# A two-block fp32 transformer kernel: ffn output halves, index order, 128-row queries, out product by token, and fp32r maxima

## The reference

```
ffn:   h = (silu(n @ w_gate) * (n @ w_up)) @ w_down        # hidden width 2816
       x = x + 0.5 * rms_norm(h, g)
mlstm: dmat[t, s] = b[t] - b[s] + i[s], -inf for s > t     # chunks of 128 tokens, 8 heads
       m[t] = max(b[t] + m_prev, max_s dmat[t, s]); p = (q k^T) * exp(dmat - m)
mix2:  p = rms_norm(x) @ w_in, split into conv (cb, cc, cx, cgate), q, k, v, agate,
           iq, ik, iw, pool (pu, pgate) and three gates of width 1024 (mgate)
       q, k = rope(rms_norm per head); iq, ik = rope
       score[t, s] = sum_h relu(iq_h[t] . ik[s] / 8) * iw[t, h] / sqrt(8), -inf for s > t
       keep the 64 largest scores of each token; softmax(q k^T / 8) over the kept keys, 8 heads of 64
       merged = sum_b sigmoid(mgate_b) * (y_b @ w_out_b); x = x + merged @ w_o
```

## Time and profile before

| | |
|---|---|
| median of 3 runs (range) | 1643.65 us (1642.29 to 1644.79) |
| the profiled execution: time, span | 1644.14 us, 1642.4 us |
| TensorE / VectorE / ScalarE / GpSimd busy | 97% / 59% / 49% / 3% of the span |
| DMA | 279.23 MB, mean 170 GB/s |
| chain that ended last, by engine | PE 76%, DVE 14%, ACT 5%, issue 2% |

### The profile page before, as it was taken

How to read it: one execution, slowest core, us unless ns; L and a number is a source line. 1 busy time by engine, 2 the same in 40 slices (tenths; PEclk the granted TensorE clock), 3 DMA queues, 4 the chain that set the end, 5 groups by cost and what they waited for, 6 DMA issues and landing times.

```text
span 1642.4 us, 19449 instructions
## 1 busy us (share of the span) xinstructions
PE 1595.2 (97%) x7539; PEld 1305.7 (80%) x7539; DVE 976.2 (59%) x1229; ACT 811.2 (49%) x1018; POOL 54.5 (3%) x97
## 2 busy tenths in 40 slices
PE   7999999899999999999999999999999999999999
PEld 6888778778887788878887888787788878778887
DVE  4555567665555645466666544567945556794564
ACT  5444465363444544456755443554355436436452
POOL 2000010000000000000000000100000000100000
PEclk9999999999999999999999999999999999999999
DMA  9644753255447463554355545563523545443443
GB/s 296 215 155 160 250 193 103 66 203 172 160 148 262 167 203 112 201 190 168 140 167 174 185 153 179 184 224 135 180 87 144 208 165 205 154 154 103 154 155 127
DMA packets 189093, 279.23 MB, mean 170 GB/s; under 512 B 8509, under 2 KB 102885, under 8 KB 189024
## 3 DMA queue, kind: packets, MB, share of 16 engines
q1 hardware_dynamic: 186752, 271.27, 47.6%
q0 software_dynamic: 2128, 6.97, 1.6%
q10 hardware_dynamic: 144, 0.03, 0.0%
HBM read 277.20 MB, written 1.06 MB: 169 GB/s over the span
## 4 chain that ended last, share of the span: by engine, by line
PE 76%; DVE 14%; ACT 5%; issue 2%; DMA 1%; POOL 1%; POOLq 0%; SPq 0%; ACTq 0%; DVEq 0%
PE ACC L770 20%; PE ACC L772 20%; PE ACC L771 20%; DVE WL L1953 5%; ACT WH L1352 2%; PE TB L801 2%; PE ZB L946 2%; PE ACC L1075 2%; PE ACC L1077 1%; PE ACC L1076 1%; ACT XH L1383 1%; PE ACC L978 1%; PE ACC L980 1%; PE ACC L979 1%; DVE IS L2467 1%
## 5 line engine op out<-in xcount | busy, mean ns | idle before, releaser
L1953 DVE TENSOR_TENSOR WL<-RAW,WH 128x2048 fp32r<-128x2048 f32 (+2 forms) x258 | 512.2, 2028 | 263.8 <-ACT WH L1352 263.8
L770 PE MATMUL ACC<-WL,XH 128*128 128x512 f32 (+2 forms) x1312 | 516.9, 394 | 20.0 <-issue 6.5
L772 PE MATMUL ACC<-WH,XL 128*128 128x512 f32 (+2 forms) x1312 | 507.1, 387 | 0.0
L771 PE MATMUL ACC<-WH,XH 128*128 128x512 f32 (+2 forms) x1312 | 506.7, 386 | 0.0
L1352 ACT ACTIVATE WH<-RAW 128x2048 fp32r<-128x2048 f32 (+2 forms) x258 | 425.7, 1701 | 154.8 <-PE ACC L772 100.4
L770 PEld LDWEIGHTS ACC<-WL,XH 128*128 128x128 f32 x1312 | 247.5, 189 | 79.5 <-issue 19.8
L772 PEld LDWEIGHTS ACC<-WH,XL 128*128 128x128 f32 x1312 | 247.3, 189 | 50.7
L771 PEld LDWEIGHTS ACC<-WH,XH 128*128 128x128 f32 x1312 | 247.8, 189 | 46.1
L770 PE MATMUL ACC<-WL,HH 128*128 128x512 f32 x352 | 138.3, 393 | 0.9 <-DVE WL L1953 0.4
L772 PE MATMUL ACC<-WH,HL 128*128 128x512 f32 x352 | 137.1, 389 | 0.0
L771 PE MATMUL ACC<-WH,HH 128*128 128x512 f32 x352 | 137.0, 389 | 0.0
(11 more groups left out here) (311 smaller groups left out, 1810.9 us busy)
## 6 DMA issues: line engine op xcount, KB each, us to landing
RAW<-w_in_in SPq DMA_DIRECT2D x66, 1024.0 KB, 6.7
RAW<-ffn_w_gate_in SPq DMA_DIRECT2D x43, 1024.0 KB, 5.2
RAW<-ffn_w_up_in SPq DMA_DIRECT2D x43, 1024.0 KB, 7.4
RAW<-ffn_w_down_in SPq DMA_DIRECT2D x32, 512.0 KB, 4.5
RAW<-ffn_w_down_in SPq DMA_DIRECT2D x16, 1024.0 KB, 6.2
RAW<-mlstm_w_in_in SPq DMA_DIRECT2D x16, 1024.0 KB, 6.9
RAW<-ffn_w_down_in SPq DMA_DIRECT2D x16, 768.0 KB, 6.1
RAW<-attn_w_in_in SPq DMA_DIRECT2D x12, 1024.0 KB, 7.0
```

What stands on the lines that cost most here:

```text
L770: nc.tensor.matmul(bank, lh, wl[:, i, :], start=first and i == 0, stop=False)
L771: nc.tensor.matmul(bank, lh, wh[:, i, :], start=False, stop=False)
L772: mm = nc.tensor.matmul(bank, ll, wh[:, i, :], start=False, stop=last and i == k - 1)
L1953: nc.vector.tensor_tensor(WL[:, slot, lo:hi], RAW[:, slot, lo:hi], WH[:, slot, lo:hi].bitcast(F32), ALU.subtract).then_inc(lo_ready, 1)
```

## The change

- ffn: `scaled` of the first output half (both tiles), and its squares, now stand before the split of chunk 6 (`postnorm_front`).
- `next_x` stands at `k - 3` of the last product instead of `k - 1` (ffn) and `k - 2` (attention, mLSTM); tile 1's transposes at `k - 3` instead of `k - 2`.
- index: the head sums of q (`norms`) and the tasks index 0 and 1 come before q's rotation. `select(1)` is cut into two tasks of four rounds, at slots 16 and 18.
- mix2 queries go to QZ2, one head per 128 rows with the other head's 64 rows zero (zeroed by GpSimd once), by four half-height evacuations instead of two; QT2 shrinks to KT2. The mask is added by VectorE into UL2, from which maxima and exponent read; PE waits for the maxima, no longer for the exponent, before the next scores.
- mix2 out product: token tile 0 of both halves is finished first, with `next_x` in two parts within tile 1; splits and adds follow in `out_tail`.
- mLSTM: MU is split into MUH and MUL on ScalarE and VectorE; identity and `after` are copied to fp32r (IDR, AFR); three fp32r matmuls take the place of two fp32 ones.

The diff without context, indentation reduced:

```diff
@@ -212,15 +212,18 @@
-QT2 = sb("QT2", [P, 3, 4, SEQ], offset=o)
-o += 3 * 4 * SEQ * 4
+KT2 = sb("KT2", [P, 2, 4, SEQ], offset=o)
+o += 2 * 4 * SEQ * 4
+UL2 = sb("UL2", [P, 2, 3 * P], offset=o)
+o += 2 * 3 * P * 4
+QZ2 = sb("QZ2", [P, HEADS, SEQ], offset=sbuf_at["G"])
-MK = sb("MK", [P, 3 * P], F32R, offset=o)
+MK = sb("MK", [P, 3 * P], offset=o)
...
@@ -434,15 +443,15 @@
-task(8, ("rotate", "q"))
+task(8, ("norms", "q"), ("index", 0), ("index", 1), ("rotate", "q"))
-task(12, ("rotate", "k"))
+task(12, ("norms", "k"), ("rotate", "k"))
-for h in range(HEADS):
+for h in range(2, HEADS):
-task(18, "conv_in")
+task(18, "conv_in", ("select", 2))
@@ -599,8 +608,7 @@
-by_half = stages[stage - 1][0] == "mix2"
-return 4 * (stage - 1) + (2 * half + tok if by_half else 2 * tok + half) + 1
+return 4 * (stage - 1) + 2 * tok + half + 1
@@ -752,7 +760,7 @@
-if fresh is not None and tok == 0 and i == k - 2:
+if fresh is not None and tok == 0 and i == k - 3:
@@ -763,7 +771,7 @@
-if tail and tok == NTOK - 1 and i == k - 1:
+if tail and tok == NTOK - 1 and i == k - 3:
@@ -777,9 +785,9 @@
-def of_x(tok, t):
-    for half in range(2):
+def of_x(tok, t, halves=range(2)):
+    for half in halves:
@@ -825,19 +833,12 @@
-def out_product(second_half=None, tok_major=False):
-    if second_half is None:
-        for half in range(2):
-            product(XH, XL, at.chunk, at.chunk % 2, at.block, at.block % 2, 0, KD, COLS, True, True,
-                    tail=next_x if half else None)
-            at.chunk += 1
-            at.block += 1
-        return
+def out_product(second_half):
-    def quarter(part, half, tok, x_at):
+    def quarter(part, half, tok, x_at=None):
@@ -848,31 +849,27 @@
+    t = slice(tok * P, (tok + 1) * P)
-        t = slice(tok * P, (tok + 1) * P)
-        if half and tok and k == x_at:
-            next_x()
+        if x_at and k in x_at and at.stage < len(stages):
+            of_x(0, at.group, (x_at[k],))
-    elif tok and half == 0 and tok_major:
+    elif tok and half == 0:
-        quarter(0, half, tok, None)
+        quarter(0, half, tok)
-if tok_major:
-    for tok in range(NTOK):
-        for half in range(2):
-            quarter(1, half, tok, KD - 2)
-else:
-    for half in range(2):
-        for tok in range(NTOK):
-            quarter(1, half, tok, KD - 1)
+quarter(1, 0, 0)
+quarter(1, 1, 0)
+quarter(1, 0, 1, {KD - 4: 0, KD - 1: 1})
+quarter(1, 1, 1)
@@ -940,12 +937,10 @@
-def head_scores(q, k, z, add=None):
+def head_scores(q, k, z):
-        mm = nc.tensor.matmul(z[:, lo:hi], q[:, queries], k[:, 0:hi - lo], start=True, stop=add is None)
-        if add:
-            mm = nc.tensor.matmul(z[:, lo:hi], add[0], add[1][:, lo:hi], start=False, stop=True)
+        mm = nc.tensor.matmul(z[:, lo:hi], q[:, queries], k[:, 0:hi - lo], start=True, stop=True)
@@ -997,7 +992,7 @@
-if half and tok and k == KD - 2:
+if half and tok and k == KD - 3:
...
@@ -1156,7 +1151,7 @@
-pe.wait_ge(gates_dve, 5)
+pe.wait_ge(largest_lo, 1)
@@ -1168,9 +1163,11 @@
-nc.tensor.matmul(m, ident[:, h:h + 1].broadcast_to([P, P]), MU[:, :], start=True, stop=False)
-nc.tensor.matmul(m.rearrange("p (c t) -> p c t", c=2), ident,
-                 after.unsqueeze(1).broadcast_to([P, 2, P]), start=False, stop=True).then_inc(z_ready, 1)
+of_head = IDR[:, h:h + 1].broadcast_to([P, P])
+nc.tensor.matmul(m, of_head, MUL[:, :], start=True, stop=False)
+nc.tensor.matmul(m, of_head, MUH[:, :], start=False, stop=False)
+nc.tensor.matmul(m.rearrange("p (c t) -> p c t", c=2), IDR[:, :],
+                 AFR[:, :].unsqueeze(1).broadcast_to([P, 2, P]), start=False, stop=True).then_inc(z_ready, 1)
@@ -1234,7 +1231,7 @@
-head_scores(QT2[halves(h), 2, h // 2, :], IKT[halves(h), :], (ZB, OB)[h % 2][:, 0:3 * P]).then_inc(index_z_ready, 1)
+head_scores(KT2[halves(h), 1, h // 2, :], IKT[halves(h), :], (ZB, OB)[h % 2][:, 0:3 * P]).then_inc(index_z_ready, 1)
@@ -1242,11 +1239,10 @@
-    pe.wait_ge(mask_ready, layer + 1)
+    pe.wait_ge(query_rows_zeroed, 2)
-    pe.wait_ge(w_ready, u0 + s)
-head_scores(QT2[halves(s), 0, s // 2, :], QT2[halves(s), 1, s // 2, :], ZB[:, 0:3 * P],
-            (IDR[:, :], MK)).then_inc(z_ready, 1)
+    pe.wait_ge(logits_ready, u0 + s)
+head_scores(QZ2[:, s, :], KT2[:, 0, s // 2, :], ZB[:, 0:3 * P]).then_inc(z_ready, 1)
...
@@ -1419,17 +1415,14 @@
-def postnorm(chunks_per_half):
-    for half in range(2):
-        b = at.block - 2 + half
-        c = at.chunk - 1 - (1 - half) * chunks_per_half
-        for tok in range(NTOK):
-            if half and tok:
-                next_x()
-            block_ready(tok, c, b)
-            square(ACC[:, pair(b) + tok, :], ST[:, tok, :], half * 2 + tok, 2)
-    at.rsqrt += 2
+def postnorm(half, last_chunk, block):
+    for tok in range(NTOK):
+        if half and tok:
+            next_x()
+        block_ready(tok, last_chunk, block)
+        square(ACC[:, pair(block) + tok, :], ST[:, tok, :], half * 2 + tok, 2)
+    at.rsqrt += half * 2
@@ -1460,10 +1453,12 @@
+    if i == len(DOWN) + 1:
+        postnorm(0, at.chunk - 2, at.block)
+postnorm(1, at.chunk - 1, at.block + 1)
-postnorm(len(DOWN))
@@ -1638,6 +1633,8 @@
+act.wait_ge(gates_dve, 4)
+nc.scalar.activation(MUH[:, :], MU[:, :], ACT.Copy).then_inc(largest_hi, 1)
@@ -1714,7 +1711,7 @@
-softmax_exp(s, ZB[:, 0:3 * P])
+softmax_exp(s, UL2[:, s % 2, :])
...
@@ -1752,7 +1749,18 @@
-tasks.update(q=lambda: plain(QT2[:, 0], DH ** -0.5), k=lambda: plain(QT2[:, 1]), iq=lambda: plain(QT2[:, 2]),
+def queries():
+    for g in range(2):
+        act.wait_ge(groups_ready, at.group + 1)
+        src = TB[at.group % 2][:, :].rearrange("p (k n) -> p k n", k=2)
+        for odd in range(2):
+            rows = slice(DH * odd, DH * odd + DH)
+            ins = nc.scalar.activation(QZ2[rows, 4 * g + odd:4 * g + 4:2, :], src[rows, :, :], ACT.Copy, scale=DH ** -0.5)
+        ins.then_inc(groups_used, 1)
+        at.group += 1
+tasks.update(q=queries, k=lambda: plain(KT2[:, 0]), iq=lambda: plain(KT2[:, 1]),
@@ -1761,13 +1769,31 @@
+def out_tail():
+    c = at.chunk + 2
+    at.front += 1
+    def next_hi(part):
+        if part == 0:
+            act.wait_ge(raw_ready[c % 2], raw_value(c))
+        act.wait_ge(weights_used if part else front_used, c if part else at.front)
+        cols = slice(part * SLOT // 2, (part + 1) * SLOT // 2)
+        nc.scalar.activation(WH[:, c % 2, cols], RAW[:, c % 2, cols], ACT.Copy).then_inc(hi_ready, 1)
+    if next_size:
+        next_hi(0)
+        x_hi(0)
+        next_hi(1)
+    at.chunk += 2
+    at.block += 2
-    if b + 1 < len(ORDER):
-        split_next(SIZES[b + 1])
-    else:
-        split_next(next_size)
-    if b == len(ORDER) - 2:
+    split_next(SIZES[b + 1])
+    if kind == "out":
+        out_tail()
+        break
...
@@ -1926,6 +1951,12 @@
+if layer == 0:
+    pool.wait_ge(rsqrts, at.rsqrt)
+    nc.gpsimd.memset(QZ2[DH:P, 0::2, :], 0.0).then_inc(query_rows_zeroed, 1)
+    pool.wait_ge(query_rows_zeroed, 1)
+    nc.gpsimd.memset(QZ2[0:DH, 1::2, :], 0.0).then_inc(query_rows_zeroed, 1)
+    pool.wait_ge(query_rows_zeroed, 2)
@@ -2044,17 +2075,20 @@
+def scaled(half, tok):
+    at.square += 1
+    dve.wait_ge(squares, at.square)
+    cols = slice(half * COLS, (half + 1) * COLS)
+    return nc.vector.tensor_tensor(XN[:, tok, cols], ACC[:, pair(at.block + half) + tok, :], G[:, at.row % 2, cols], ALU.mult)
+def postnorm_front():
+    dve.wait_ge(row_loaded[at.row % 2], 16 * (at.row // 2 + 1))
+    scaled(0, 0)
+    scaled(0, 1).then_inc(blocks_used, 1)
-    row = at.row % 2
-    dve.wait_ge(row_loaded[row], 16 * (at.row // 2 + 1))
-    at.row += 1
-    def scaled(half, tok):
-        at.square += 1
-        dve.wait_ge(squares, at.square)
-        cols = slice(half * COLS, (half + 1) * COLS)
-        return nc.vector.tensor_tensor(XN[:, tok, cols], ACC[:, pair(at.block - 2 + half) + tok, :], G[:, row, cols], ALU.mult)
@@ -2064,12 +2098,12 @@
-scaled(0, 0)
-scaled(0, 1).then_inc(blocks_used, 1)
+at.row += 1
+at.block += 2
@@ -2108,10 +2142,11 @@
-for size in DOWN_SIZES[1:] + [next_size]:
+for i, size in enumerate(DOWN_SIZES[1:] + [next_size]):
+    if i == len(DOWN) + 1:
+        postnorm_front()
-at.block += 2
@@ -2238,6 +2273,8 @@
+step(nc.vector.tensor_copy(IDR[:, :], ident))
+step(nc.vector.tensor_copy(AFR[:, :], after))
@@ -2309,6 +2346,8 @@
+dve.wait_ge(largest_hi, 1)
+nc.vector.tensor_tensor(MUL[:, :], MU[:, :], MUH[:, :].bitcast(F32), ALU.subtract).then_inc(largest_lo, 1)
...
@@ -2395,8 +2433,6 @@
-nc.vector.tensor_reduce(HN[:, :], SQ[:, :, :].rearrange("p t (h e) -> p (t h) e", e=DH), AX_X, ALU.add)                            .then_inc(head_sums, 1)
-at.head_norm += 1
@@ -2414,6 +2450,13 @@
+def norms(kind):
+    dve.wait_ge(blocks_used, b0 + ORDER.index(kind) + 2)
+    dve.wait_ge(rope_done, at.staged)
+    nc.vector.tensor_reduce(HN[:, :], SQ[:, :, :].rearrange("p t (h e) -> p (t h) e", e=DH), AX_X, ALU.add)\
+        .then_inc(head_sums, 1)
+    at.head_norm += 1
@@ -2452,22 +2495,25 @@
-def select(tok):
+def select(part):
```

(83 more changed lines are left out.)

## The result

| kernel | median us (range, runs) | ratio to the kernel before, 95% interval |
|---|---|---|
| before | 1643.01 (1642.29 to 1644.79, 4) | |
| changed | 1620.32 (1618.21 to 1620.81, 4) | 0.9857 [0.9845, 0.9868] |
| changed, in a later batch | 1619.86 (1617.90 to 1621.03, 4) | 0.9855 [0.9838, 0.9871] |

The change is faster by 23 us; forecast were 37, with a range that ended at 1618. The profiled execution of the changed kernel took 1618.21 us (span 1616.3), that of the later batch 1619.02 (1617.2).

What follows compares the result with a forecast made beforehand. The prediction took TensorE, busy 97% of the span, as the bound. Its terms, 8.0 + 0.6 + 1.4 + 4.0 + 19.9 + 3.9 = 37.8 us off 1644.14, gave 1606.3, forecast as 1606; range 1600 to 1612, with rivals 1598 to 1618.

Steps and rivals of the forecast that it cites:

- four ffn exits: Ends of the four ffn stages: earlier transposes of X nearly close TensorE's 1.31 us hole; 2.0 us each, 8.0 in all.
- start, attention and mLSTM exits: Transposes one k step earlier: 0.6 us at the kernel's start, 1.4 at the ends of attention and mLSTM.
- mLSTM maxima: mLSTM: three fp32r matmuls instead of two fp32 ones save 0.50 us a head, eight heads, 4.0.
- index: mix2 index work: heads 4 and 5 run together without their wait, 2.3 us per layer; with the clock 6.2 together.
- selection, and give-back at cb: mix2: halved selection removes the wait before "pu", 3.1 us; about 1.3 per layer is lost before "cb".
- units, less the wait at unit 2: mix2 scores: padded queries without mask matmuls save 0.96 us in sixteen units, 15.4; unit 2 loses 1.1 per layer.
- between the layers: Boundary of the mix2 layers: the 1.99 us stall and the low clock behind it go; 3.9 us saved.
- What is given back in mix2: mix2, VectorE nearly full: TensorE arrives early and waits about 1.3 us per layer at "cb", 1.1 at unit 2.
- rival 2: Clock falls at the new stalls (cb, unit 2, two layers), 1.2 to 1.6 us each: 1611 to 1612; chance 0.07.
- Rival 1: VectorE and ScalarE bound all of mix2, which then brings about 9 us: 1617; chance 0.18.
- Rival 3: mix2 scores: padded queries cost what 64-row ones did, only the mask leaves; 7.7 us less, 1614; chance 0.05.
- The last sign of being wrong: mix2: the prediction is wrong if waits on VectorE sum to much over 5 us.

Runs made afterwards that it cites:

- exits_only: The kernel before with only the change's ffn exits and earlier next-X transposes, also in attention and mLSTM: 1632.48 us against 1643.7.
- relu_first: The changed kernel with ScalarE's relus of index heads 6 and 7 ahead of the mix2 query evacuation: 1620.71 us.
- select_split: The changed kernel with 4 of 8 rounds of the first token tile's selection, and the mask, behind the next split in both mix2 layers: 1620.47 us.
- unit_first: The changed kernel with unit work ahead of the next chunk's split, slot 22 on ScalarE and VectorE, slot 26 on VectorE: 1611.47 us.

## Why the prediction was wrong

By its own steps, from landmarks of the trace of 1619.02 (which is 25.1 of 37.8 ahead of before at the last product):

| step | forecast | measured |
|---|---|---|
| four ffn exits | 8.0 | 7.9 |
| start, attention and mLSTM exits | 2.0 | 2.4 |
| mLSTM maxima | 4.0 | 1.3 |
| index | 6.2 | 2.4 + 3.9 |
| selection, and give-back at cb | 3.1 - 2.6 | 3.3 - 3.2 |
| units, less the wait at unit 2 | 15.4 - 2.2 | 3.3 a layer, 6.6 |
| clock behind the new wait | 0 | -2.9 |
| between the layers | 3.9 | 4.4 |
| later start of q in layer 2 | 0 | -1.1 |

- Exits, index and layer boundary: right in mechanism and size; exits_only measures the first by itself.
- The wait before cb was forecast (1.3, measured 1.39), but not its cause: I put it on ScalarE's four query evacuations; relu_first shows that they don't matter, select_split that VectorE's queue does. Selection and give-back are one sum on a full VectorE, not two terms.
- **The step that failed most: "What is given back in mix2", the wait at unit 2.** I looked only at the logits' chain, found 1.1, and missed that the transposes also need a bank which ScalarE frees behind its split: 2.76 and 0.76 a layer. "Units are 5.4 us or more apart" was true and didn't help, as the wait was not for the unit's own chain. Of the difference of 3.3 a layer 2.4 are these waits. Another 0.6 is that I took 0.96 for each of eight units: five save it, the three whose scores stand behind other 128-column matmuls save 0.83 to 0.92, and behind each of the two waits the transposes come another 0.16 later. About 0.3 isn't assigned.
- The clock: rival 2 (0.07) was half right. The clock did fall, by 2.9, the second largest term; but behind the wait of 2.76 that it didn't name, and not behind cb's 1.39 that it did. And I took it for a rival to the forecast where it was a part of it.
- "mLSTM maxima": 0.43 saved a head instead of 0.50, and the walk through TensorE's next wait, done for mix2, was left out here. The cover, "two projections away", was that of the added copies, not of the scores.
- "Later start of q in layer 2": TensorE waits 0.82 for the weights' low half (0.90 in the first profile). ScalarE's split starts late there, as it waits 1.47 for the chunk's transfer (0.29 before; the row is from the trace of 1619.02). The forecast walked to the end of the boundary and not on to this chunk. Why the transfer doesn't keep up with the earlier TensorE wasn't tried.

```profile
1351.81 3.72 ACT L1348 ACTIVATE WH<-RAW 128x2048 fp32r<-128x2048 f32 x2 [1.47 <-DMA RAW<-w_in_in]
```

- Rival 1 (1617) was half right: VectorE bounds the entrance, but in the units it is the order, as unit_first shows. Its 9 us for mix2 is just what came (6.3 + 0.1 + 6.6 - 2.9 - 1.1 = 9.0), but by luck: it had the index bringing nothing. Rival 3 fell: 64 rows cost more by themselves, and more still in turns.
- The last sign of being wrong, waits on VectorE in mix2 much over 5 us, did not catch this: they sum to 5.5 in the first profile, and 6.2 more are on ScalarE, which it doesn't watch.

Sum of the misses: 2.7 (mLSTM) + 6.6 (units) + 2.9 (clock) + 1.1 ("q") = 13.3, less 0.5 by which the other steps together came out better = 12.8, for 37.8 - 25.1 = 12.7.

## What to carry over

When TensorE comes earlier, list for its next instructions every buffer that they need, the bank they write to as well as the data they read, and look at what stands ahead of its last reader on that engine; a long split ahead of a short evacuation is the first thing to turn round, on every engine that has one there. Price a new stall of the length of these with the clock behind it: 16 of 18 of 2.4 us and more inside mix2 had half clock behind them. A gain at a place where another engine is 96% busy is not a gain until that engine has less to do.

## What I had not expected of the hardware

- 64-row score matmuls on their own, between 128-row ones, were slower than zero-padded 128-row ones by 0.29 a unit of four records, and with 128-row matmuls in between by 0.74 more than the padded form with the same mask matmuls (1.85 against 1.11).
- The same program with the same wait of 2.7 to 2.8 had its clock halved behind it in both layers of one profiled execution and in neither of the other. This makes 3.0 us between them; their times differ by 0.8 only, because the one with the falls was 2.1 ahead when it came to the first wait.
